# One decoder step (convolution, latent attention, memory attention, experts): caches and memory keys turned by the host layout, sample scores issued a pair ahead

## The reference

```python
h = rmsnorm(x); proj = h @ w_in          # value 512 | gate 512 | q latent 384 | kv latent 256 | rotary key 32
u = val * sigmoid(gate); conv = causal depthwise conv of width 31 (+ 30 rows of state per sequence)
conv_out = silu(layernorm(conv))
q = rmsnorm(q_in) @ w_q_up               # 8 heads, 64 + 32 rotary
q_lat = einsum(q_nope, w_uk)             # attention in the latent space
s = (q_lat . ckv + q_pe . kpe) * scale   # ckv, kpe: the sequence's cache of 1024 tokens in 8 pages of 128
                                         # (found by page_table), and the new tokens
attn_out = (softmax(s) . ckv) . w_uv
x += concat(conv_out, attn_out) @ w_out
m = rmsnorm(mem_prompt); k, v = m @ w_mk, m @ w_mv            # prompt's memory; the samples' is cached
x += memory_attend(rmsnorm(x), k, v) @ w_mo                   # 4 heads of 128 over 256 memory tokens
x += top-4-of-32 experts with clamped SwiGLU; final rmsnorm
```

## Time and profile before

| | |
|---|---|
| time, median of 3 executions (lowest, highest) | 1313.5 us (1312.72, 1314.37) |
| profiled execution, span from first to last instruction | 1310.9 us |
| left around the span (median less span) | 2.6 us |
| busy in the span: PE, DVE, ACT, POOL | 1250.0, 515.0, 210.6, 15.5 us |
| transfers: mean rate, bytes | 344 GB/s, 451.38 MB |

### The profile page before, as it was taken

How to read it: one execution, slowest core, us unless ns; L and a number is a source line. 1 busy time by engine, 2 the same in 40 slices (tenths; PEclk the granted TensorE clock), 3 DMA queues, 4 the chain that set the end, 5 groups by cost and what they waited for, 6 DMA issues and landing times.

```text
span 1310.9 us, 15428 instructions
## 1 busy us (share of the span) xinstructions
PE 1250.0 (95%) x5954; PEld 518.9 (40%) x5954; DVE 515.0 (39%) x1223; ACT 210.6 (16%) x434; POOL 15.5 (1%) x20
## 2 busy tenths in 40 slices
PE   7999898999999999999999999999999999999996
PEld 4665654556533333333333333333333333333331
DVE  1168778334453233422323332223333323334224
ACT  3014433313411011010001000101000011010111
POOL 0100010000000000000000000000000000000000
PEclk9999899999999999999999999999999999999999
DMA  9701123391699999999999999999999999999994
GB/s 345 294 12 43 36 79 131 104 414 59 244 397 396 425 427 425 426 426 427 427 428 427 427 427 426 427 428 426 427 426 399 387 424 427 425 428 424 425 426 194
DMA packets 43599, 451.38 MB, mean 344 GB/s; under 512 B 5222, under 2 KB 6182, under 8 KB 17940
## 3 DMA queue, kind: packets, MB, share of 16 engines
q1 hardware_dynamic: 42012, 441.22, 80.7%
q0 software_dynamic: 1536, 9.44, 1.9%
...
HBM read 447.72 MB, written 3.28 MB: 344 GB/s over the span
## 4 chain that ended last, share of the span: by engine, by line
PE 74%; DMA 19%; DVE 5%; ACT 1%; issue 1%; SPq 0%; DVEq 0%
PE psum L916 38%; DMA ring<-in_w_up 16%; PE psum L337 6%; PE psum L898 5%; PE psum L962 4%; PE psum L425 3%; DMA ring<-in_w_gate 2%; PE psum L644 2%; DVE ring L1756 1%; PE psum L767 1%; PE psum L403 1%; PE psum L946 1%; PE psum L615 1%; PE psum L773 1%; PE psum L378 1%; PE psum L385 1%
## 5 line engine op out<-in xcount | busy, mean ns | idle before, releaser
L916 PE MATMUL psum<-ring,work 128*64 128x512 f32 x3072 | 676.9, 595 | 21.2 <-DMA ring<-in_w_up 19.5
L916 PEld LDWEIGHTS psum<-ring,work 128*64 128x64 f32 x3072 | 216.4, 137 | 469.9 <-issue 416.8
L898 PE MATMUL psum<-H,work 128*64 128x512 f32 (+1 forms) x384 | 92.7, 600 | 0.0
L2169 DVE TENSOR_TENSOR work<-psum,keep 128x512 f32<-128x512 f32 x16 | 11.1, 692 | 165.9 <-PE psum L916 165.9
L2155 DVE TENSOR_TENSOR X<-X,psum 128x512 f32<-128x512 f32 x68 | 46.7, 686 | 67.4 <-PE psum L962 67.3
L1756 DVE SCALAR_TENSOR_TENSOR ring<-ring,cwT 128x256 f32<-128x256 f32 x240 | 72.5, 377 | 0.1
L2169 DVE TENSOR_TENSOR work<-psum,work 128x512 f32<-128x512 f32 x16 | 11.1, 692 | 141.6 <-PE psum L916 141.4
L1604 ACT COPY work<-psum 64x512 f32<-64x512 f32 x32 | 18.5, 578 | 298.2 <-PE psum L916 298.2
L1592 ACT COPY work<-psum 128x512 f32<-128x512 f32 x31 | 18.2, 587 | 278.8 <-PE psum L898 278.8
L337 PE MATMUL psum<-C,work 128*128 128x128 f32 (+5 forms) x360 | 55.1, 286 | 5.6 <-DMA work<-in_small_rows 3.8
L337 PEld LDWEIGHTS psum<-C,work 128*128 128x128 f32 (+5 forms) x360 | 47.2, 186 | 30.9 <-issue 21.8
...
## 6 DMA issues: line engine op xcount, KB each, us to landing
...
```

The source lines that it names most:

```text
L898: last = mm(psum[64 * nh:64 * nh + 64, 2, :], Ph[0:ROWS[tt], tt, :], xn[0:ROWS[tt], tt, 512 * nh:512 * nh + 512], start=tt == 0, stop=tt == 2)
L916: last = mm(psum[64 * nh:64 * nh + 64, bank, :], src[:, j, 64 * half:64 * half + 64], w[:, half, j, 512 * nh:512 * nh + 512], start=first ...
L2169: v.tensor_tensor(gm, psum[:, 0, :], B[b][:, 0:512], ALU.add).then_inc(s.g_sum, 1)
```

## The change

The host lays out what the kernel flipped: the vectors (with the taps of the convolution) as columns, the memory tokens, the conv state and w_uk turned, the cached memory keys with head dimension on partitions, and the paged cache twice: `cache_keys` holds for each page 128 rows of 288 numbers (both halves of the latent turned, 32 rotary numbers of four token groups), `cache_values` holds rows of 8 tokens as before. Memory tokens are also loaded as rows, for the mean squares. So `sa_flip`, `ms_keys`, the flips of vectors, memory tokens, state and w_uk and the copies of their results go. POOL loads keys with 8 indirect transfers for a sequence (one for each page) and values with one. `sa_scores` works on four banks of 256 columns; its rotary part uses queries copied into four groups of 32 partitions (two copies by DVE, two by ACT, and DVE waits for ACT's). Scores of pairs 0 and 1 are issued before the pair loop, those of pair p + 2 after the values of pair p; DVE's scale and maximum likewise. ACT scales half of the scores. The memory values' products move behind gate and value. ACT takes the mean squares of x before those of the memory tokens. More taps lie before the attention, fewer in the pairs. The mean-subtracted result of the convolution is scaled into another buffer, and SP's third part of w_out waits for that scaling instead of for the activation.

```diff
-CONV_EARLY = (5, 10, 10)
+CONV_EARLY = (11, 12, 12)
...
-            pe.wait_ge(s.load_ident, 32)
...
-            for tt in range(2):
-                if tt == 0:
-                    pe.wait_ge(s.load_mem, 16)
-                for kk in range(2):
-                    ps = V.open(pe, ("mT", tt, kk))
-                    for k in range(4):
-                        last = flip(ps[:, 128 * k:128 * k + 128], mem[:, tt, 128 * (4 * kk + k):128 * (4 * kk + k + 1)], P)
-                    last.then_inc(s.full_v, 1)
-            emptied(pe, V, ("mT", 1, 1))
             pe.wait_ge(s.load_wmk, 16)
-            keys = [A.open(pe, ("mk", tt)) for tt in range(2)]
+            pe.wait_ge(s.mem_scaled, 1)
+            mem_keys = [A.open(pe, ("mk", tt)) for tt in range(2)]
             for k0 in (0, 4):
                 if k0:
                     pe.wait_ge(s.load_wmk2, 16)
+                    pe.wait_ge(s.mem_scaled, 2)
                 for tt in range(2):
+                    if k0 and tt:
+                        flip_tile("hT", 0, 0, by_block)
                     for k in range(k0, k0 + 4):
-                        last = mm(keys[tt], mT[:, k, 128 * tt:128 * tt + 128], wmk[:, k, :], start=k == 0, stop=k == KD - 1)
+                        last = mm(mem_keys[tt], mT[:, k, 128 * tt:128 * tt + 128], wmk[:, k, :], start=k == 0, stop=k == KD - 1)
                     if k0:
                         last.then_inc(s.full_a, 1)
+            for tt in range(1, 3):
+                flip_tile("hT", 0, tt, by_block)
+            pe.wait_ge(s.load_lat, 16)
+            for tt in range(2):
+                emptied(pe, V, ("hT", tt, 1))
+                for lane, name, c0, n in ((A, "qlat", 2 * CH, QR), (V, "kvlat", 2 * CH + QR, KR + ROPE)):
+                    ps = lane.open(pe, (name, tt))
+                    for k in range(KD):
+                        last = mm(ps[:, 0:n], hT[:, k, tok(tt)], w_in[:, k, c0:c0 + n], start=k == 0, stop=k == KD - 1)
+                    last.then_inc(lane.full, 1)
...
-            def sa_flip(b):
-                pe.wait_ge(cache_in[b % 4], 32 * (b // 4 + 1))
-                for ct in range(2):
-                    for g in range(2):
-                        lane = (V, A)[ct]
-                        ps = lane.open(pe, ("cT", b, ct, g))
-                        for j in range(4):
-                            last = flip(ps[:, 128 * j:128 * j + 128], cache[b % 4][:, 4 * g + j, 128 * ct:128 * ct + 128], P)
-                        last.then_inc(lane.full, 1)
-                for g in range(2):
-                    ps = A.open(pe, ("pT", b, g))
-                    for j in range(4):
-                        last = flip(ps[0:32, 128 * j:128 * j + 128], cachep[b % 4][:, 4 * g + j, :], P)
-                    last.then_inc(s.full_a, 1)
             def sa_scores(pair):
                 emptied(pe, V, ("qlT", 1))
-                for g in range(2):
-                    ps = V.open(pe, ("sa_s", pair, g))
-                    for k in range(3):
+                lanes = (V, V, A, A)
+                quad = [lanes[g].open(pe, ("sa_s", pair, g)) for g in range(4)]
+                for b2 in range(2):
+                    b = 2 * pair + b2
+                    pe.wait_ge(key_in[b % 5], 128 * (b // 5 + 1))
+                for k in range(2):
+                    for g in range(4):
                         for b2 in range(2):
                             b = 2 * pair + b2
-                            if g == 0 and k == 0:
-                                emptied(pe, V, ("cT", b, 0, 1))
-                                emptied(pe, A, ("pT", b, 1))
-                            out = ps[64 * b2:64 * b2 + 64, :]
-                            if k < 2:
-                                last = mm(out, qlT[:, k, 64 * b:64 * b + 64], cT[b2][:, k, 512 * g:512 * g + 512],
-                                          start=k == 0, stop=False)
-                            else:
-                                last = mm(out, qpeT[:, b, :], pT[b2][0:32, 512 * g:512 * g + 512], start=False, stop=True)
-                    last.then_inc(s.full_v, 1)
-                ps = V.open(pe, ("sa_s", pair, 2))
+                            mm(quad[g][64 * b2:64 * b2 + 64, 0:256], qlT[:, k, 64 * b:64 * b + 64],
+                               keys[b % 5][:, :, PAGE * k + 32 * g:PAGE * k + 32 * g + 32], start=k == 0, stop=False)
+                for g in range(4):
+                    for b2 in range(2):
+                        b = 2 * pair + b2
+                        last = mm(quad[g][64 * b2:64 * b2 + 64, 0:256], qpeT[32 * g:32 * g + 32, b, :],
+                                  keys[b % 5][32 * g:32 * g + 32, :, 2 * PAGE:KREC], start=False, stop=True)
+                    if g != 1:
+                        last.then_inc(lanes[g].full, 1)
...
             latent_queries()
+            sa_scores(0)
             pa_turn(0)
-            sa_flip(0)
+            sa_scores(1)
             pa_turn(1)
-            sa_flip(1)
             for pair in range(4):
-                sa_scores(pair)
+                sa_turn(pair)
                 pa_values(pair)
                 if pair < 3:
                     pa_scores(2 * pair + 2)
-                    sa_flip(2 * pair + 2)
                     pa_scores(2 * pair + 3)
+                else:
+                    ln_mean()
+                sa_values(pair)
+                if pair < 2:
+                    sa_scores(pair + 2)
+                if pair < 3:
                     pa_turn(2 * pair + 2)
                 else:
                     pe.wait_ge(s.load_wout, 16)
                     emptied(pe, V, ("pa_o", 3))
                     first = [S.open(pe, ("out", 0, nh)) for nh in range(2)]
-                    for nh in range(2):
-                        out_part(first[nh], 0, nh, (4, 5, 6, 7))
-                sa_turn(pair)
-                if pair == 3:
-                    ln_mean()
-                sa_values(pair)
-                if pair == 3:
+                    out_part(first[0], 0, 0, (4, 5, 6, 7))
                     ln_var()
-                if pair < 3:
-                    sa_flip(2 * pair + 3)
                 sa_flip_out(pair)
                 if pair < 3:
                     pa_turn(2 * pair + 3)
+                else:
+                    out_part(first[1], 0, 1, (4, 5, 6, 7))
...
-            ms_keys(1)
             ma_values(0)
+            ma_scores(3)
             ms_scores(0)
-            ma_scores(3)
-            ms_keys(2)
+            ms_scores(1)
             ma_values(1)
             ma_turn(2)
-            ms_scores(1)
-            ms_keys(3)
             ms_scores(2)
+            ms_scores(3)
             ma_values(2)
-            ms_keys(4)
-            ms_scores(3)
+            ms_scores(4)
             ma_turn(3)
-            ms_keys(5)
-            ms_scores(4)
+            ms_scores(5)
+            ms_scores(6)
             ma_values(3)
-            ms_keys(6)
-            ms_scores(5)
-            ms_keys(7)
-            ms_scores(6)
             pe.wait_ge(s.load_wmo, 16)
...
-            dma(C[:, 0:128], a["constants"][:, 0:128]).then_inc(s.load_ident, 16)
-            dma(small_rows, a["small_rows"]).then_inc(s.load_ident, 16)
-            dma(mem, a["mem_prompt"][0].rearrange("(t p) d -> p t d", p=P)).then_inc(s.load_mem, 16)
+            dma(vecT[:, :], a["vectors"]).then_inc(s.load_vec, 16)
+            dma(mT[:, 0:4, :], a["mem_turned"][:, 0:4, :]).then_inc(s.load_mem, 16)
             dma(wmk[:, 0:4, :], rows_of(a["w_mk"][0])[:, 0:4, :]).then_inc(s.load_wmk, 16)
+            dma(mT[:, 4:8, :], a["mem_turned"][:, 4:8, :]).then_inc(s.load_mem2, 16)
             dma(wmk[:, 4:8, :], rows_of(a["w_mk"][0])[:, 4:8, :]).then_inc(s.load_wmk2, 16)
+            dma(C[:, 0:128], a["constants"][:, 0:128]).then_inc(s.load_x, 16)
             dma(X[:, 0:2, :], a["x_prompt"][0].rearrange("(t p) d -> p t d", p=P)).then_inc(s.load_x, 16)
             dma(X[0:NS, 2, :], a["x_sample"].rearrange("b t d -> (b t) d")).then_inc(s.load_x, 16)
+            dma(w_in[:, :, 2 * CH:], rows_of(a["w_in"][0])[:, :, 2 * CH:]).then_inc(s.load_lat, 16)
+            dma(mem, a["mem_prompt"][0].rearrange("(t p) d -> p t d", p=P)).then_inc(s.load_rows, 16)
+            dma(w_in[:, :, 0:2 * CH], rows_of(a["w_in"][0])[:, :, 0:2 * CH]).then_inc(s.load_win, 16)
...
-            dma(page[:, :], a["page_rows"]).then_inc(s.load_pages, 16)
+            dma(page[:, :], a["page_rows"]).then_inc(s.load_const, 16)
+            dma(UC[:, :, SEQ + 30:SEQ + 30 + 8 * (WIDTH - 1)], a["state_turned"]).then_inc(s.load_state, 16)
+            produced(sp, A, ("mk", 1))
             dma(wmv, rows_of(a["w_mv"][0])).then_inc(s.load_wmv, 16)
-            dma(w_in[:, :, 2 * CH:], rows_of(a["w_in"][0])[:, :, 2 * CH:]).then_inc(s.load_lat, 16)
-            dma(w_in[:, :, 0:2 * CH], rows_of(a["w_in"][0])[:, :, 0:2 * CH]).then_inc(s.load_win, 16)
```

(80 more changed lines are left out.)

388 lines of the change are left out of this document (170 added, 218 removed).

## The result

The changed kernel took **1326.03 us** (median of 4 executions, 1325.01 to 1327.19) beside 1313.11 us before (4 executions): ratio 1.0095, 95% interval 1.0081 to 1.0109, so 0.95% slower. The forecast was 1282 us, range 1270 to 1296, with a chance of 0.92 for faster. Later the same kernel took 1282.69 us on one chip and 1321.09 us on another (the last experiments), so the document has to explain two times, not one. The profile shown here is of the first measurement, with a span of 1324.9 us.

What follows compares the result with a forecast made beforehand. The expert loop runs at the weight stream's pace, so only its earlier start counts: span 1310.9 less 32.9 gained plus 2 for the clock is 1280; with 2.6 around it 1282.6, said as 1282, range 1270 to 1296.

Steps and rivals of the forecast that it cites:

- Each indirect transfer keeps its queue for 1.25 us: POOL's key and value loads: each issue occupies POOL's queue 1.25 us and lands 4.7 to 5.9 us after issue.
- POOL becomes the bound: Rival: POOL's key issues slow down; above 2.2 us each the whole gain goes, at 2.5 the time is 1329; chance 0.05.
- fourth scores start (wait for keys 7): Attention's last pair: PE waits 6.4 us until the last of the final sequence's keys lands at 177.7 us.
- sa_v ends: End of the sample outputs, after attention and convolution: at 223.1 us instead of 249.90, a gain of 26.8 us so far.
- Start: 0 to 68 us and on to q: flips go, memory values move behind gates; q starts at 104.6, gain 3.0 us.
- the new wait for x: Before the latent projection: PE waits 3.5 us for the first normalised tile of x, as ScalarE is late.
- Scores of a pair: Attention: latent, rotary and new-token products of one pair take 5.4 us (4.8 to 6.3), before 6.4; rotary part 1.1.
- Keys and values late: Attention pairs: POOL's transfers arrive late, giving PE new waits of 0.7, 1.7 and 6.4 us.
- POOL keeps up: Rival: shorter key transfers remove 8 us of waits, and row groups running together save 1 to 2: 1273; chance 0.2.
- Memory attention: Before the output product: 56 flips of cached keys leave an unbroken PE stretch, gaining 6.1 us (3 to 6.1).
- The rule against the change: POOL beside DVE: two-port operations shut GpSimd out, so issues would pass 2.2 us; the forecast kept 1.25 from the rows.
- the 2 us charged for the clock: Attention and convolution: PE's clock at 1.2 instead of 2.4 GHz behind the new waits costs 2 us (0 to 5).

Runs made afterwards that it cites:

- chip S: The changed kernel, run again unchanged on another chip: 1282.69 us in one execution, beside 1314.75 for the kernel before.
- keys by SP: Changed kernel, but keys issued by SP as plain transfers with page numbers in registers, values still gathered by POOL: 1275.15 us, ratio 0.9708.
- P, R and T: Chips. P and R: kernel before plus sixteen POOL gathers at 54 us, 1319.09 (P), 1319.10 and 1319.55 us (R); T: changed kernel unchanged, 1321.09 us.
- 16 in a row: Kernel before plus sixteen back-to-back POOL gathers at 54 us: 1319.10 us with 256-byte rows, 1319.55 us with 1024-byte rows from eight index columns.
- 8 + 8: Kernel before plus two runs of eight POOL gathers of 1024-byte rows from 54 us, POOL waiting between them for the first eight to land: 1312.17 us.
- the kernels that were to test them: Kernel before plus 16, 8, 4 or 16 POOL gathers, begun at other times relative to instruction packets: 1312.19, 1315.57, 1314.83 and 1312.99 us.

## Why the prediction was wrong

**The step that failed** is the price of POOL's transfers: "Each indirect transfer keeps its queue for 1.25 us" and nothing else. I charged 72 issues to POOL's own queue and to those who wait for their data, and held the rest of the machine to be untouched. The spacing is right: its median is 1.25 us with and without hold-ups (single ones reach 1.58 and 1.52). What was missing is that a run of them delays TensorE's semaphore increments to ScalarE and VectorE, by 2 to 12 us, on some chips. None of the rivals was that. The nearest in time, "POOL becomes the bound" at 1329 us, came out near the measured time for a wrong reason: its p had to pass 2.2 us.

That this, and not the rest of the sum, is the error, the execution without hold-ups shows, step by step (us):

| step | predicted | held, first measurement | not held, chip S | keys by SP, chip P |
|---|---|---|---|---|
| latent projection starts | 28.6 | 30.0 | 30.5 | 29.8 |
| gates start | 52.3 | 53.6 | 54.1 | 53.3 |
| q starts | 104.6 | 119.7 | 106.4 | 105.6 |
| prompt attention starts | 129.3 | 151.5 | 131.0 | 130.2 |
| fourth scores start (wait for keys 7) | 177.7 (6.4) | 220.8 (none) | 178.8 (4.3) | 173.1 (1.3) |
| sa_v ends | 223.1 | 267.3 | 224.6 | 218.9 |
| time | 1282 | 1326.0 | 1282.7 | 1275.2 |

- *Start.* The first product came at 9.9 on chip S, not 8.1, and x landed at 19.5, not "at 17.0 as before" (18.9 in the held kernel); the new wait for x is there, 1.8 to 2.3 us, not 3.5. Then q is 1.8 late on the forecast, and 1.5 of it is left at the end of sa_v.
- *Loss in the held kernel.* 13.3 us are lost by q (119.65 less 106.40), 20.4 by the first prompt scores, 42.0 by the fourth scores, 42.7 by the end of sa_v. All of the 43 us between 1326.0 and 1282.7 is there. Part of it is PE's lower clock (0.75 in 133 to 250 us against 0.94 on chip S): the 24 matmuls of q, at 0.84 against 1.00, take 9.51 in place of 7.98 us. That follows the idling and is no cause of its own, as it is gone with the hold-ups.
- *Scores of a pair.* The rotary part in four row groups goes from start to start in 0.62 us (168.18 to 168.80 in the changed kernel), where two times 1.0 stood; my 1.1 was too high. The Trainium skill, "TensorEngine Tiling (Array Packing)", "Theoretical Speedup", gave up to four times, and the trace nearly agrees (2.0 to 0.62). A pair whose clock and banks are there takes 4.9 us on chip S (144.18 to 149.05) and not 5.4.
- *Keys and values late.* Predicted waits 0.7, 1.7 and 6.4; on chip S none, 3.3 and 4.3. With keys by SP these shrink to 1.3, and sa_v ends 5.7 us sooner. That is the rival "POOL keeps up" (1273), reached by another issuer: 1275.2 measured.
- *Memory attention.* SP's release of the expert weights moved from 340.81 to 310.51 on chip S: 30.3 us against 32.9 predicted; less the 25.3 at the end of sa_v, the stage gave 5.0, not 6.1.
- *The rule against the change.* POOL's issues stay 1.25 us apart beside VectorE's taps. The Trainium skill, "SBUF — State Buffer", "SBUF: two separate sides", would have had them stretched if the taps shut GpSimd out, as by that page VectorE's two-port operations do; no such stretch is in the trace, with POOL at 1.25 us.

The range 1270 to 1296 held for chip S and misses the first measurement by 30 us. That chip S comes within 1 us of 1282 is in part luck. Of the span (1280.7 against 1280.0 summed), sa_v is 1.5 late and the memory attention gave 1.1 less; the 2 us charged for the clock take that back, for it was 0.94 in 133 to 250 us, as before the change.

**What stays open.** Why long runs of gathers delay TensorE's increments and on which chips. It is shown for P, R and T, by different kernels; on P the changed kernel itself was not run. It is not shown whether a length, or something that must fall into the run, is needed: on R 16 in a row do it and 8 + 8 do not, but in the changed kernel runs of eight do (169.8 to 179.5 us). The packets of instructions are ruled out as a need only for the hold-ups of some 2 to 3 us at 140 us; for the longer ones they stay open, as the kernels that were to test them ran on S. A chip and what was loaded on it were never told apart, and chip S ran the changed kernel once. All executions with a time here also had their records taken; whether the effect is there without, no run tells.
